# Two decay products ahead of the previous pair's output in a state-space loop

## The chip, the cores and the metric

The kernel runs on one core of one Trainium2 chip. The metric is the device time of one execution in microseconds (us). The engines are TensorE (PE in the rows; PEld is its weight load), VectorE (DVE), ScalarE (ACT), GpSimd (POOL) and SyncE (SP), which issues the weight transfers. Each runs its own instructions in order, and they meet through semaphores.

## The reference, cut to what matters

Two different transformer blocks are computed one after the other, each two layers deep, on 512 positions of width 1024, in float32. Block 1 mixes sliding-window attention, forgetting attention and a state-space part, and then attends to a memory. The change is in the state-space part, in the piece that the reference writes so:

```python
diff = acs[:, :, :, None] - acs[:, :, None, :]
decay = jnp.exp(jnp.where(causal[:, :, None, None], diff, NEG_INF))
cb = jnp.einsum('bclgn,bcsgn->bclsg', cm, bm)
y_diag = jnp.einsum('bclsg,bclsgh,bcsghp->bclghp', cb, decay, xs)
...
y_off = jnp.einsum('bclgn,bcghpn,bclgh->bclghp', cm, prev, jnp.exp(acs))
return (y_diag + y_off).reshape(b, s, h, p)
```

`acs` is a running sum over each chunk of 128 positions, there are 4 chunks and 16 heads of width 64, in two groups of 8. Behind it come the skip term `d_skip * xs` and a gate `silu(z)`.

## The kernel before

The five engines have a program each. In block 1, `first_layer(l)` of each engine runs twice. The state-space loop is `for t in range(HEADS // 2)`: eight turns, one for each pair of heads 2t and 2t+1. It has no scheduler: each engine's order is the order in which its code is written. All sizes are 128 partitions by 512 (4 chunks by 128) for one head, if nothing else is said.

What one turn t does, by engine:

- **TensorE** (from line 2168) waits until the first difference of pair t has been read out of its bank (`spread_read`), then broadcasts the running sums of pair t+1 to all partitions, one head to a bank (`broadcast_sums`, two of them; the banks are 0, 1 and 6 in turn, and the operand has 16 rows), then multiplies four 512 KB units of a weight matrix that has nothing to do with this loop (`mod_unit`, the modulation of block 2, 16 matmul records a unit, 64 in a turn), then waits twice for `operand_ready`, that is for the decay products of both heads, and makes the pair's output (28 matmul records that read `work`, `levels` and `h_sb`) in bank 4 or 5.
- **ScalarE** (lines 2386, 2371 and 2393) takes the exponential of the broadcast sums of both heads into `e_off` (two instructions of 128x384), copies the finished group of modulation rows of turn t-1 out of its bank (line 2371), and then takes the exponential of both heads' differences in place, four instructions of 128x128 for a head, eight in all (line 2393). It begins a head's four when VectorE has made that head's difference.
- **VectorE** makes, for each head of the pair, `c_off` (line 2641: `e_off` times the C matrix, 128x384) and the difference `diff` (line 2643: bank minus the token's own sum, cut at it). Then, if t is not 0, it does `pair_out(t - 1)`, the output of the pair before: line 2625 adds the skip term to bank 4 or 5 and frees the bank, line 2627 multiplies by the gate. Then `decay_keyed` (line 2635) for both heads: the exponential of the difference times `cbm`, into `m_dec`, which TensorE's output matmuls read. The buffers of `e_off` and `diff` are two, one for each head of a pair; those of `c_off` and `m_dec` are four, of which the fourth is in the tile `levels`, so that its rows read `levels<-...`. The eighth pair's output follows behind the loop.

The waits of `decay_keyed` are on `act_output`, which ScalarE raises when a head's four exponentials are done. `pair_out` waits for TensorE's output matmuls of the pair that it treats.

```python
def decay_keyed(hh):
    await_(act_output)
    me.link(V.tensor_tensor(m_dec[hh % 4], diff[:, hh % 2, :], cbm[:, hh // 8, :], ALU.mult), operand_ready)
```

The weights come in one stream of 512 KB units into a ring of eight slots. SyncE issues the load of a slot when TensorE has begun the unit that follows the slot's old one. Behind the loop TensorE goes on with the output projection of block 1, from tiles that are ready since long, and comes to the state-space result only four units later.

Of the kernel before, what the change touches and what calls it, by code (L numbers as in the profile page):

```python
# [51 lines left out]
def build(nc, names, out):  # L52
# [4 lines left out]
    with ctx:  # L57
# [2375 lines left out]
        def _(dve):  # L2433
# [6 lines left out]
            def await_(s):  # L2440
                dve.wait_ge(s, me.nth(s))
# [75 lines left out]
            def first_layer(l):  # L2517
# [105 lines left out]
                def pair_out(t):  # L2623
                    bank_full()
                    me.link(V.scalar_tensor_tensor(out=gtmp, in0=xbc[:, t, :], scalar=par1(l, A_SKIP + t),
                                                   in1=banks[4 + t % 2][:, :], op0=ALU.mult, op1=ALU.add), freed_by_dve)
                    me.link(V.tensor_tensor(y[:, 8 + t, :], y[:, 8 + t, :], gtmp, ALU.mult))
# [5 lines left out]
# [4 lines that stand above are left out]
                for t in range(HEADS // 2):  # L2637
                    for hh in (2 * t, 2 * t + 1):
                        r, g = hh % 2, hh // 8
                        await_(act_output)  # L2640
                        me.link(V.tensor_tensor(c_off[hh % 4][:, P:T], xbc[:, 10 + g, P:T], e_off[:, r, P:T], ALU.mult),
                                wait=False)
                        me.link(V.tensor_tensor(chunked(diff[:, r, :]), chunked(banks[SUM_BANKS[hh % 3]][:, :]), acs_tok(hh),  # L2643
                                                ALU.min), spread_read, wait=False)
                    if t:
                        pair_out(t - 1)
                    for hh in (2 * t, 2 * t + 1):
                        decay_keyed(hh)
                def input_sums(v, sums, last=True):

                    t1, t2, t3, t4 = sums
                    low, high = v[:, 0:4, :], v[:, 4:8, :]
                    me.link(V.tensor_tensor(t1, low[:, :, SECOND], low[:, :, FIRST], ALU.subtract))
                    me.link(V.tensor_tensor(t2, high[:, :, SECOND], t1, ALU.subtract))
                    me.link(V.tensor_tensor(t3, high[:, :, SECOND], low[:, :, SECOND], ALU.subtract), wait=False)
                    me.link(V.tensor_tensor(t4, high[:, :, FIRST], t2, ALU.subtract), operand_ready if last else None)
# [74 lines left out]
            for l in range(DEPTH):  # L2731
                first_layer(l)
# [221 lines left out]
```

How the kernel before makes its waits and increments, by code:

```python
            def link(self, ins, s=None, wait=True):  # L232
                s = s or self.step
                self.done[s.name] = self.done.get(s.name, 0) + 1
                ins.then_inc(s, 1)
                if wait:
                    self.eng.wait_ge(s, self.done[s.name])
# [124 lines left out]
        @block.sync  # L363
# [4 lines left out]
            sp.dma_start(x[:, 0:2, 0:T], x_pairs(names["xT"], 0)).then_inc(x_in[0], 16)
            sp.dma_start(const[:, 0:C_LEVEL], names["consts"][:, 0:C_LEVEL]).then_inc(first_consts_in, 16)
            for n in range(1, 4):
                sp.dma_start(x[:, 2 * n:2 * n + 2, 0:T], x_pairs(names["xT"], n)).then_inc(x_in[n], 16)
            sp.dma_start(par[:, :], names["params"]).then_inc(params_in, 16)
            unit = 0
            for blk, l, phase in ORDER:
                if blk == 2 and l == 0 and phase == "na":
                    sp.wait_ge(memory_read, DEPTH)
                    sp.dma_start(x[:, :, T:ALL], names["ctxT"].rearrange("(k p) t -> p k t", p=P)).then_inc(ctx_in, 16)
                    sp.dma_start(cst(C_TAB, 2 * ALL), names["tables2"]).then_inc(ctx_in, 16)
                for n in range(UNITS[phase]):
                    if phase == "na" and n == 6:
                        sp.wait_ge(table_room, l + 1)
                        if l:
                            sp.dma_start(cst(C_TAB, 2 * ALL), names["tables2"]).then_inc(rope_in, 16)
                        sp.dma_start(work[:, RPB_AT:RPB_AT + RPB_WIDTH], names["bias"][l]).then_inc(table_in, 16)
```

## Time and profile before

| what | value |
|---|---|
| three runs | 3464.1, 3467.82 and 3470.92 us, median 3467.82 us |
| the profiled execution | 3461.59 us, of which the span of its instructions is 3459.8 us |
| TensorE busy | 3284.1 us (95%) |
| VectorE busy | 1147.1 us (33%) |
| ScalarE busy | 973.8 us (28%) |
| GpSimd busy | 330.9 us (10%) |
| bytes moved | 437.69 MB, mean 127 GB/s |
| the state-space loop of layer 0 | from 447.18 us (first `c_off`) to 491.83 us (the last pair's output matmuls are over) |
| that of layer 1 | from 1236.38 us to 1281.51 us |

Times inside the trace are microseconds from the start of the span. The sum below is made against the profiled execution, 3461.59 us.

### The profile page before, as it was taken

The page shows a single profiled execution, that of the slowest core. Times are in us where ns is not written, and L with a number is a line of the kernel's source. Part 1 is how long each engine was busy: PE and PEld are TensorE (multiplying, and loading weights), DVE is VectorE, ACT ScalarE, POOL GpSimd, SP SyncE. Part 2 cuts the span into 40 slices and gives each one's busy share as a digit, 9 for nine tenths or more (in the row PEclk, how much of TensorE's full clock was granted, in tenths as well). Part 3 has the DMA queues.
Part 4 walks back from the last instruction along what each step waited for, and adds up shares of the span by engine and source line. Part 5 has one row for each costly group of instructions (what it writes and reads, how often), then busy time and mean ns, then how long its engine had stood idle before and what let it go on. Part 6 is the DMA issues. An engine that isn't in the chain of part 4 may idle for free.

```text
span 3459.8 us, 46188 instructions
## 1 busy us (share of the span) xinstructions
PE 3284.1 (95%) x19102; PEld 1942.4 (56%) x19102; DVE 1147.1 (33%) x2497; ACT 973.8 (28%) x2072; POOL 330.9 (10%) x336
## 2 busy tenths in 40 slices
PE   8999999999999999999999999979989999997999
PEld 4464457875464456876755777533325756663333
DVE  2224454142224464133352456130002344453011
ACT  1345140111335141114232354121113234442110
POOL 0000002110000002110000064011000000430000
PEclk9999999999999999999999999989999999997999
DMA  4221372312221272422101000169993111014997
GB/s 155 98 74 55 104 264 83 123 44 73 67 80 49 75 297 67 134 68 83 43 25 43 13 2 32 61 233 367 360 335 114 43 32 42 1 62 146 396 409 306
DMA packets 120270, 437.69 MB, mean 127 GB/s; under 512 B 13168, under 2 KB 15344, under 8 KB 119424
## 3 DMA queue, kind: packets, MB, share of 16 engines
q1 hardware_dynamic: 113040, 407.45, 32.3%
q0 software_dynamic: 7024, 27.30, 2.4%
q8 instruction: 153, 2.51, 0.3%
q14 instruction: 53, 0.43, 0.0%
HBM read 422.08 MB, written 12.62 MB: 126 GB/s over the span
## 4 chain that ended last, share of the span: by engine, by line
PE 87%; DVE 5%; DMA 3%; ACT 3%; issue 1%; SPq 0%; POOL 0%; DVEq 0%; ACTq 0%; POOLq 0%
PE bank L1880 85%; DMA ring<-in_stream 2%; PE bank L2025 1%; ACT work L2288 1%; DMA h_sb<-in_stream 1%; PE bank L914 0%; DVE work L2469 0%; DVE work L2471 0%; ACT h_sb L2393 0%; DVE work L1631 0%; DMA work<-in_stream 0%; PE bank L2128 0%; DMA work<-tokens,slot_tok 0%; DVE small L1630 0%; DVE work L2498 0%
## 5 line engine op out<-in xcount | busy, mean ns | idle before, releaser
L1880 PE MATMUL bank<-h_sb,ring 128*128 128x512 f32 (+2 forms) x3104 | 1183.7, 536 | 22.5 <-ACT h_sb L1139 10.8
L1880 PEld LDWEIGHTS bank<-h_sb,ring 128*128 128x128 f32 (+1 forms) x3104 | 570.1, 189 | 533.1 <-issue 487.6
L1880 PE MATMUL bank<-y_sb,ring 128*128 128x512 f32 (+1 forms) x928 | 329.4, 512 | 3.3 <-DVEq L230 3.3
L2248 ACT ACTIVATE work<-bank 128x512 f32<-128x512 f32 (+1 forms) x250 | 124.8, 509 | 709.0 <-PE bank L1880 616.3
L1880 PE MATMUL bank<-work 128*64 128x128 f32 (+6 forms) x1936 | 282.0, 347 | 17.0 <-ACT work L2288 4.7
L1880 PE MATMUL bank<-ring,h_sb 128*128 128x128 f32 (+2 forms) x2144 | 284.8, 311 | 1.4 <-ACT work L1302 0.7
L1880 PEld LDWEIGHTS bank<-y_sb,ring 128*128 128x128 f32 x928 | 175.3, 190 | 151.0 <-issue 138.5
L1880 PEld LDWEIGHTS bank<-ring,h_sb 128*128 128x128 f32 (+2 forms) x2144 | 232.2, 185 | 42.3 <-issue 39.2
L1880 PEld LDWEIGHTS bank<-work 128*64 128x64 f32 (+2 forms) x1936 | 181.7, 163 | 93.7 <-issue 57.4
L1880 PE MATMUL bank<-ring,work 128*64 128x512 f32 (+2 forms) x920 | 223.9, 559 | 4.1 <-DMA ring<-in_stream 4.0
L1880 PE MATMUL bank<-y_sb,work 128*64 128x128 f32 (+3 forms) x984 | 185.3, 435 | 1.0 <-DMA work<-in_stream 0.8
L2288 ACT ACTIVATE work<-work,small 128x256 f32<-128x256 f32 (+4 forms) x188 | 109.0, 580 | 194.2 <-DVEq L230 194.0
L2248 ACT ACTIVATE y_sb<-bank 128x512 f32<-128x512 f32 (+1 forms) x163 | 87.0, 557 | 197.5 <-PE bank L1880 173.9
L1880 PEld LDWEIGHTS bank<-ring,work 128*64 128x64 f32 (+1 forms) x920 | 63.7, 130 | 106.0 <-issue 105.3
L1880 PEld LDWEIGHTS bank<-y_sb,work 128*64 128x64 f32 (+2 forms) x984 | 73.8, 137 | 72.2 <-issue 65.7
L1880 PE MATMUL bank<-work,const 64*128 64x128 f32 (+4 forms) x440 | 101.4, 419 | 6.8 <-DVE h_sb L2643 3.7
L2259 ACT ACTIVATE h_sb<-x_sb 128x1024 f32<-128x1024 f32 (+1 forms) x56 | 47.4, 895 | 206.6 <-DVEq L230 200.6
L2025 PEld LDWEIGHTS bank<-const,work 128*128 128x128 f32 x576 | 68.9, 141 | 58.7 <-issue 39.6
L1880 PE MATMUL bank<-work,y_sb 128*64 128x64 f32 (+1 forms) x400 | 96.1, 391 | 4.4 <-issue 2.9
L1770 POOL TENSOR_TENSOR work<-ring 128x512 f32<-128x512 f32 x14 | 18.5, 1324 | 825.3 <-DMA ring<-in_stream 777.0
L2025 PE MATMUL bank<-const,work 128*128 128x128 f32 x576 | 84.6, 275 | 12.2 <-ACT y_sb L2248 11.4
L1880 PE MATMUL bank<-h_sb,work 128*64 128x128 f32 (+3 forms) x544 | 90.1, 372 | 5.0 <-issue 3.7
(322 smaller groups left out, 3674.7 us busy)
## 6 DMA issues: line engine op xcount, KB each, us to landing
ring<-in_stream SPq DMA_DIRECT2D x578, 512.0 KB, 5.1
y_sb<-in_stream SPq DMA_DIRECT2D x110, 512.0 KB, 7.1
h_sb<-in_stream SPq DMA_DIRECT2D x40, 512.0 KB, 14.9
work<-in_stream SPq DMA_DIRECT2D x20, 512.0 KB, 15.3
work<-in_bias SPq DMA_DIRECT2D x2, 2688.0 KB, 9.8
tokens<-work POOLq DMA_DIRECT2D x10, 512.0 KB, 4.1
work<-forget POOLq DMA_DIRECT2D x2, 1536.0 KB, 7.1
x_sb<-in_xT SPq DMA_DIRECT2D x4, 512.0 KB, 5.9
```

Of the source, the lines that this page charges most:

```text
L1770: me.link(V.tensor_tensor(s3, a11, a21, ALU.subtract), weight_sums)
L1880: return nc.tensor.matmul(o, a, b, start=first, stop=last, skip_group_check=True)
L2025: ins = nc.tensor.transpose(banks[b][:, j * P:(j + 1) * P], scores_in(i - 1, s)[:, kb * P:(kb + 1) * P], ident)
L2248: me.link(A(o, i, func, **kw), freed_by_act, wait=False)
L2259: me.link(A(dst[:, k:k + 2, :], src[:, k:k + 2, :], ACT.Square), squares_ready, wait=False)
L2288: me.link(A(at, banks[s][:, 0:u["nk"]] if raw else at, ACT.Exp, bias=nmax[:, j:j + 1], scale=1.0 if raw else -1.0, accum_out=rsum[:, j:j + ...
```

## The change

Inside a turn of the loop, VectorE's two `decay_keyed` are written ahead of `pair_out(t - 1)` instead of behind it. Nothing is added or removed, and no other engine's program changes. The first turn, which has no `pair_out`, and the part behind the loop stay as they are.

```diff
@@ -2642,10 +2642,10 @@
                         me.link(V.tensor_tensor(chunked(diff[:, r, :]), chunked(banks[SUM_BANKS[hh % 3]][:, :]), acs_tok(hh),
                                                 ALU.min), spread_read, wait=False)
+                    for hh in (2 * t, 2 * t + 1):
+                        decay_keyed(hh)
                     if t:
                         pair_out(t - 1)
-                    for hh in (2 * t, 2 * t + 1):
-                        decay_keyed(hh)
```

VectorE's queue in the second turn (pair 1) of layer 0 and the beginning of the third, before. The bank at the end of an input tells the rows of line 2625 apart (bank 4 is pair 0's output, bank 5 is pair 1's):

```order
L2641 TENSOR_TENSOR levels<-work,h_sb 128x384
L2643 TENSOR_TENSOR h_sb<-bank0,small 128x512
L2625 SCALAR_TENSOR_TENSOR work<-work,par,bank4 128x512
L2627 TENSOR_TENSOR y_sb<-y_sb,work 128x512
L2635 TENSOR_TENSOR work<-h_sb,cpad 128x512
L2635 TENSOR_TENSOR levels<-h_sb,cpad 128x512
L2641 TENSOR_TENSOR work<-work,h_sb 128x384
L2643 TENSOR_TENSOR h_sb<-bank1,small 128x512
```

The same place with the change:

```order
L2641 TENSOR_TENSOR levels<-work,h_sb 128x384
L2643 TENSOR_TENSOR h_sb<-bank0,small 128x512
L2635 TENSOR_TENSOR work<-h_sb,cpad 128x512
L2635 TENSOR_TENSOR levels<-h_sb,cpad 128x512
L2625 SCALAR_TENSOR_TENSOR work<-work,par,bank4 128x512
L2627 TENSOR_TENSOR y_sb<-y_sb,work 128x512
L2641 TENSOR_TENSOR work<-work,h_sb 128x384
L2643 TENSOR_TENSOR h_sb<-bank1,small 128x512
```

The two rows of line 2635 have moved ahead of the two of pair 0's output, and these now stand directly ahead of the next pair's `c_off` and difference.

The end of the loop in layer 0, from the last pair's second difference on, before:

```order
L2643 TENSOR_TENSOR h_sb<-bank0,small 128x512
L2625 SCALAR_TENSOR_TENSOR work<-work,par,bank4 128x512
L2627 TENSOR_TENSOR y_sb<-y_sb,work 128x512
L2635 TENSOR_TENSOR work<-h_sb,cpad 128x512
L2635 TENSOR_TENSOR levels<-h_sb,cpad 128x512
L2625 SCALAR_TENSOR_TENSOR work<-work,par,bank5 128x512
L2627 TENSOR_TENSOR y_sb<-y_sb,work 128x512
```

The same place with the change:

```order
L2643 TENSOR_TENSOR h_sb<-bank0,small 128x512
L2635 TENSOR_TENSOR work<-h_sb,cpad 128x512
L2635 TENSOR_TENSOR levels<-h_sb,cpad 128x512
L2625 SCALAR_TENSOR_TENSOR work<-work,par,bank4 128x512
L2627 TENSOR_TENSOR y_sb<-y_sb,work 128x512
L2625 SCALAR_TENSOR_TENSOR work<-work,par,bank5 128x512
L2627 TENSOR_TENSOR y_sb<-y_sb,work 128x512
```

Here too the last two decay products come first, and the outputs of pairs 6 and 7 (banks 4 and 5) follow each other.

## Rows read from the trace of the kernel before

**Rows 1.** Busy time of the engines, and shares of the chain that ended last
```profile
PE 3284.1 (95%) x19102; PEld 1942.4 (56%) x19102; DVE 1147.1 (33%) x2497; ACT 973.8 (28%) x2072; POOL 330.9 (10%) x336
...
PE 87%; DVE 5%; DMA 3%; ACT 3%; issue 1%; SPq 0%; POOL 0%; DVEq 0%; ACTq 0%; POOLq 0%
```
**Rows 2.** The chain through the loop of layer 0: start us, us, what
```profile
460.14 2.46 ACT h_sb L2393 x8
462.60 0.70 DVE work L2635
...
463.31 0.70 DVE work L2635
...
464.04 0.56 DVE work L2641
464.60 0.61 DVE h_sb L2643
...
465.23 2.46 ACT h_sb L2393 x8
...
472.37 6.84 DMA ring<-in_stream
```
**Rows 3.** VectorE in order of time, pair 2 of layer 0: start us, us, what
```profile
461.09 0.74 DVE L2625 SCALAR_TENSOR_TENSOR work<-work,par,bank 128x512 f32<-128x512 f32 x1
461.86 0.69 DVE L2627 TENSOR_TENSOR y_sb<-y_sb,work 128x512 f32<-128x512 f32 x1
462.59 1.42 DVE L2635 TENSOR_TENSOR work<-h_sb,cpad 128x512 f32<-128x512 f32 x2
```
**Rows 4.** TensorE in order of time, pair 2 and the next broadcasts
```profile
461.75 1.95 PE L1880 MATMUL bank<-ring,cond 128*32 128x128 f32 x64
464.11 0.66 PE L1880 MATMUL bank<-work 128*64 128x128 f32 x8 [0.41 <-DVE work L2635]
...
465.79 1.13 PE L1880 MATMUL bank<-work,const 16*128 16x512 f32 x4
```
**Rows 5.** Stretches, layer 0: us, PE, PEld, DVE, ACT, POOL busy, granted clock, DMA
```profile
444.40:448.40 4.00, 2.12 (x12) 0.49 (x13) 1.22 (x3) 0.89 (x3) 0.00 (x0) 0.90 0.76 270
448.40:453.40 5.00, 5.00 (x61) 3.27 (x65) 4.14 (x8) 3.17 (x10) 0.00 (x0) 0.50 0.28 87
...
458.90:464.00 5.10, 4.69 (x96) 3.52 (x96) 4.96 (x9) 4.03 (x12) 0.00 (x0) 1.00 0.99 373
...
484.60:489.70 5.10, 3.98 (x96) 3.07 (x97) 4.97 (x8) 3.04 (x9) 0.00 (x0) 1.00 1.03 408
```
**Rows 6.** ScalarE and then VectorE in order of time, pair 1 of layer 0
```profile
454.83 2.45 ACT L2393 ACTIVATE h_sb<-h_sb,small 128x128 f32<-128x128 f32 x8
...
457.49 0.69 DVE L2635 TENSOR_TENSOR work<-h_sb,cpad 128x512 f32<-128x512 f32 x1
```
**Rows 7.** ScalarE in order of time, pairs 1 and 2 of layer 1
```profile
1243.94 2.44 ACT L2393 ACTIVATE h_sb<-h_sb,small 128x128 f32<-128x128 f32 x8
...
1249.03 2.45 ACT L2393 ACTIVATE h_sb<-h_sb,small 128x128 f32<-128x128 f32 x8 [0.60 <-DVE h_sb L2643]
```
**Rows 8.** TensorE in order of time, the last pair of layer 0, then of layer 1
```profile
489.58 0.64 PE L1880 MATMUL bank<-ring,cond 128*32 128x128 f32 x16 [0.62 <-DMA ring<-in_stream]
490.15 0.32 PE L1880 MATMUL bank<-work 128*64 128x128 f32 x1
...
492.83 3.70 PE L1880 MATMUL bank<-y_sb,ring 128*128 128x512 f32 x8
...
1279.83 0.32 PE L1880 MATMUL bank<-work 128*64 128x128 f32 x1
```
**Rows 9.** TensorE in order of time, pair 0 of layer 0
```profile
448.40 2.08 PE L1880 MATMUL bank<-work,const 16*128 16x512 f32 x4 [1.84 <-DVE h_sb L2643]
450.41 3.64 PE L1880 MATMUL bank<-ring,cond 128*32 128x128 f32 x64
```
**Rows 10.** A stretch ahead of the loop of layer 1, columns as in rows 5
```profile
1219.00:1226.00 7.00, 5.17 (x61) 2.63 (x59) 5.25 (x9) 0.74 (x2) 0.00 (x0) 1.00 0.56 200
```

## The prediction

> **What bounds the kernel now.** I first read the engines' busy time and the chain that ended last. TensorE is busy for 95% of the span and stands for 87% of the chain; VectorE is 5% of the chain [rows 1]. So nearly everywhere VectorE's order is worth nothing, and the question is whether the loop of the change is one of the exceptions. The chain of waits through that loop says that it is. From 460.14 us it leaves TensorE altogether and goes in a circle: eight exponentials on ScalarE (2.46), two decay products of line 2635 on VectorE, then line 2641 and line 2643 of the next pair's first head, and at 465.23 the next eight exponentials [rows 2]. One circle, 465.23 - 460.14 = 5.09 us, is one pair of heads.
>
> Then VectorE's own timeline, to see whether the circle is tight because of a dependency or because VectorE has no time left. It is both. `pair_out` runs from 461.09 to 462.59, where the first decay product starts [rows 3], and ScalarE ends its eighth exponential at 460.14 + 2.46 = 462.60 [rows 2]. So `pair_out` (1.50 us) lies exactly beside the exponentials, and costs the circle nothing. VectorE's busy time in such a pair is 4.96 of 5.10 us [rows 5]; its work of one pair fills the period.
>
> Who else could set the pace? TensorE is busy 4.69 of 5.10 us [rows 5] and waits 0.41 us for the decay products before the pair's output [rows 4]. The DMA engines are busy at a share of 0.99 in pair 2 and 1.03 in the last pairs [rows 5], the chain goes over to the weight stream at 472.37 [rows 2], and the last modulation unit of the loop waits 0.62 us for it [rows 8]. So three things run within some 0.1 us of each other: VectorE with ScalarE, and, toward the end, the weight stream.
>
> **The change part by part.** No instruction is added or removed, TensorE's, ScalarE's and SyncE's queues are the same, and VectorE's semaphores are awaited in the same order. What moves is 1.50 us of `pair_out`, from ahead of the two decay products to behind them, in seven turns of each of two layers.
>
> *The decay products.* Counted from the start of the exponentials, the first head's are done after half of 2.46, that is 1.23, and its product could start there; the second head's after 2.46. VectorE's second difference ends 461.09 - 460.14 = 0.95 after that start [rows 2, 3]. It then idles 0.28 us, makes the first product (0.70), idles until 2.46, and makes the second (0.72 with the gap behind it, from two neighbouring starts, 463.31 and 464.04). TensorE has both at 3.16 after the start of the exponentials, where before it had them at 464.01 - 460.14 = 3.87 [rows 2, 3]. That is earlier by 0.7 within the turn, and it takes the 0.41 wait away from TensorE.
>
> *pair_out.* It now starts at 3.18 and takes its 1.50 us [rows 3], and only then does the next pair's first head start: from line 2641 to the exponentials 465.23 - 464.04 = 1.19 [rows 2]. The new circle is 2.46 + 0.72 + 1.50 + 1.19 = 5.87 us, against 5.09: longer by 0.78, which is the `pair_out` that has come into it (1.50) less the first product that has gone out of it (0.72). The same from the other side: VectorE has work for the old 5.09 and now idles 0.78 in each turn, because the 1.50 us that bridged its wait for the exponentials have gone elsewhere.
>
> *How many turns count, layer 0.* Pair 0 is unchanged. In pair 1 the exponentials start at 454.83 and take 2.45 [rows 6]; they are held by TensorE's modulation group there, not by VectorE, so this start stays. The second product can start at 457.28, against a first one at 457.49 before [rows 6]. Then 457.28 + 0.72 + 1.50 + 1.19 = 460.69 for pair 2's exponentials, against 460.14 [rows 2]. Five more circles, for pairs 3 to 7, give 460.69 + 5 x 5.87 = 490.04, the second product of pair 7 is ready at 490.04 + 2.46 + 0.70 = 493.20, and TensorE starts behind it by the 0.10 that lies between 464.01 and 464.11 [rows 3, 4]: 493.30. Before, it started at 490.15 [rows 8]. That is **+3.15 us**.
>
> *Layer 1.* Exponentials of pair 1 at 1243.94, of pair 2 at 1249.03 [rows 7]. New: 1243.94 + 2.44 + 0.72 + 1.50 + 1.19 = 1249.79 for pair 2, then 5 x 5.87 = 29.35, then 3.16 and 0.10: 1282.40, against 1279.83 [rows 8]. That is **+2.57 us**.
>
> *What takes no part.* The last `pair_out` of the loop (pair 6) ends about 1.5 us behind the last product, and pair 7's output matmuls take some 1.7 us (490.15 to 491.83, the end in the table of times), so pair 7's output is hardly held. Behind the loop TensorE goes on at once with the projection, eight matmuls of 3.70 us for a unit [rows 8], far slower than the stream brings units, so no DMA wait takes the delay back, and it stays in the end time in full. The stream itself needs 5.10 to 5.2 us for four units in the loop; at 5.87 a pair it is no longer waited for. Its part in the old end is small: VectorE's fifth circle would have given TensorE its operands at about 460.14 + 5 x 5.09 + 3.87 + 0.10 = 489.56 instead of 490.15 [rows 2, 3, 8], so 0.6 us of the loss is hidden already, and this is in the sums above.
>
> Sum: 3.15 + 2.57 = **+5.7 us**. On the profiled execution, 3461.59, this gives 3467.3. That execution lies 6.2 us below the median of the three runs (3467.82), so on the median's footing the forecast is 3467.8 + 5.7 = **3473.5 us**. A change of under 0.2%, 6.9 us, can hardly be told from none in this kernel.
>
> *A rule that points the other way.* The row shows TensorE waiting 0.41 us for line 2635 in a pair [rows 4]. The Trainium skill, Perfetto Trace Analysis, section Identifying Performance Opportunities (Optimization Strategy), says to find the gaps of the engine that limits, look who releases them, and make that dependency start sooner; this change does just that. By that rule the gap goes and the sum is a gain, where the circle of rows 2 makes it a loss.
>
> **The rivals.**
>
> *A. The products reach TensorE sooner and the loop gets shorter.* For it: such a wait stands in two pairs of each layer before the weight stream takes over, at most 0.41 us [rows 4]. Worked out: 2 x 0.41 x 2 = 1.6 us less, 3466.2. Against: it needs the circle of rows 2 not to lengthen, that is, `pair_out` behind the products hidden by something, and in those rows nothing lies beside lines 2641 and 2643 but VectorE itself.
>
> *B. The weight stream paces the loop in both orders.* For it: DMA shares of 0.99 to 1.03 and TensorE's waits for the ring near the end [rows 5, 8]. Then the end of the loop stays where it is: about 0, 3467.8. Against: 5 x 0.78 = 3.9 us more on VectorE is much more than the 0.6 us by which the stream is late.
>
> *C. TensorE's clock falls inside the loop: slower than can be overlooked.* The granted clock fell from 2.4 to 1.2 GHz (1.00 to 0.50) at the loop's beginning, behind a stretch in which TensorE was busy 2.12 of 4.00 us, the last of it a wait of 1.84 [rows 5, 9]. It stayed at 2.4 GHz while TensorE was busy 4.69 of 5.10 [rows 5], and also at 5.17 of 7.00, 74% [rows 10]. With the change TensorE works 4.69 of 5.87, 80%, and its idle time, 1.2 us, is one piece behind the pair's output. The price: at 1.2 GHz the two broadcasts and the modulation group take 2.08 + 3.64 [rows 9] instead of 1.13 + 1.95 [rows 4]. In a middle pair most of that fits into the 1.2 us of slack, over two pairs. It decides when it hits the last pair: TensorE is then 0.5 us late for the output and runs up to 5 us of the projection at half speed, as long as it lasted in rows 5, which costs up to 2.5. With some 2.2 us a layer this gives 5.7 + 4.4 = 10.1, 3477.9. A fall in every pair (2.08 + 3.64 + the output's 1.7 = 7.4 us for a pair) would cost 7 x (7.4 - 5.87) = 10.7 us a layer and end near 3495; the 80% speaks against it.
> The Trainium skill, TensorE: Matmul & The Clock Gate, Part 1, holds that the slow clock is the state at rest and that activity lifts it; that is the mechanism of this rival, and it doesn't say whether 80% in this mix is enough. The rows lean to enough.
>
> **How the numbers follow.** The longer circle with nothing more: chance 0.68, 3473.5, with a range of its own from 3470.5 to 3477 for the drift between executions (the runs spread over 6.8 us). Some of that range lies beyond 6.9 us over the median: of the 0.68 I give 0.48 to no change that can be told and 0.20 to slower. A: 0.07, of which 0.02 would show as faster. B: 0.13, all within 0.2%. C: 0.12, of which 0.11 slower. In all faster 0.02, same 0.67 (0.48 + 0.05 + 0.13 + 0.01), slower 0.31. The range must take in most of C above (3477.9) and B below (3467.8, less a little drift): 3466 to 3480. It leaves out the heavy form of C.
>
> **What would show it.** In the changed trace: VectorE's line 2635 in two separate rows with an idle time of about 0.5 us before the second, put down to ScalarE's line 2393; `pair_out` directly behind it; starts of the eight exponentials 5.87 us apart from pair 2 to pair 7 in both layers, about 490.0 and 1279 plus the shift for the last; no wait of TensorE for line 2635 over 0.2 us, but one of about 1 us before the broadcasts, put down to line 2643; its waits for the ring gone from the last pairs; the DMA share in the loop down to about 0.9. I am wrong if the period is still 5.1 (the exponentials or `pair_out` would have been hidden after all), if the last output matmuls start at the old distance from the loop's start (B), if the granted clock shows 0.5 in a stretch of the loop beyond pair 1 (C), or if the loop is longer by 5 to 6 us in all and the whole is not, which would mean that something later takes it back.

## The result, and the profile after

Over 17 runs the changed kernel took 3475.57 us in the median (3468.44 to 3479.72); 17 runs of the kernel before had a median of 3466.3 us (3458.79 to 3474.45). The ratio is 1.0024 with a 95% interval of 1.0017 to 1.0031: slower by 8.3 us, between 5.9 and 10.7 (the medians themselves are 9.3 us apart). The profiled execution has a span of 3470.6 us, against 3459.8.

The page, with busy times, the chain by engine and the chain by line (what answers to [rows 1]):

```profile
PE 3289.4 (95%) x19102; PEld 1944.6 (56%) x19102; DVE 1148.1 (33%) x2497; ACT 972.5 (28%) x2072; POOL 330.6 (10%) x336
...
PE 87%; DVE 5%; ACT 3%; DMA 2%; issue 1%; SPq 0%; DVEq 0%; POOL 0%; ACTq 0%; POOLq 0%
PE bank L1880 84%; PE bank L2025 1%; ACT h_sb L2393 1%; DMA ring<-in_stream 1%; PE bank L914 1%; DMA h_sb<-in_stream 1%; ACT work L2288 0%; DVE work L2469 0%; DVE work L2471 0%; DVE work L1631 0%; DMA work<-in_stream 0%; DVE small L1630 0%; PE bank L2128 0%; DVE work L2498 0%; DMA work<-tokens,slot_tok 0%
```

The busy times agree with those of before to within 0.2%. In the chain, ScalarE's line 2393, the exponentials of the loop, has come up from 0% to 1%, and DMA has gone from 3% to 2%. The chain of waits through the loop of layer 0 (start us, us, what) shows why, beside [rows 2]:

```profile
459.78 2.45 ACT h_sb L2393 x8
462.24 0.03 issue
462.26 0.02 DVEq L2441
462.28 0.04 issue
462.33 0.70 DVE work L2635
...
463.05 0.76 DVE work L2625
...
463.84 0.70 DVE y_sb L2627
...
464.56 0.56 DVE work L2641
465.12 0.61 DVE h_sb L2643
...
465.76 2.45 ACT h_sb L2393 x8
...
493.01 33.32 PE bank L1880 x118
```

The circle holds one decay product instead of two, and both instructions of `pair_out`. One turn is 465.76 - 459.78 = 5.98 us, against 5.09. It goes round like this up to pair 7, without passing over to the weight stream. What the prediction's circle did not have are the first three lines under the exponentials: 0.09 us from ScalarE's end to VectorE's start.

VectorE in order of time in the same pair (start us, us, engine, line, operation; idle before in brackets), against [rows 3]:

```profile
461.09 0.69 DVE L2635 TENSOR_TENSOR work<-h_sb,cpad 128x512 f32<-128x512 f32 x1 [0.28 <-ACT h_sb L2393]
462.33 0.69 DVE L2635 TENSOR_TENSOR work<-h_sb,cpad 128x512 f32<-128x512 f32 x1 [0.55 <-ACT h_sb L2393]
463.05 0.75 DVE L2625 SCALAR_TENSOR_TENSOR work<-work,par,bank 128x512 f32<-128x512 f32 x1
463.84 0.69 DVE L2627 TENSOR_TENSOR y_sb<-y_sb,work 128x512 f32<-128x512 f32 x1
```

The two products are apart, with idle times of 0.28 and 0.55 us, both put down to line 2393. Their sum, 0.83, is the greater part of the 0.89 us by which a turn is longer.

TensorE (as [rows 4] and [rows 8]): the next broadcasts, the output of pair 3, and the output of the last pair:

```profile
465.78 1.13 PE L1880 MATMUL bank<-work,const 16*128 16x512 f32 x4 [0.91 <-DVE h_sb L2643]
...
469.10 0.29 PE L1880 MATMUL bank<-work 128*64 128x128 f32 x1 [0.31 <-DVE levels L2635]
...
493.01 0.29 PE L1880 MATMUL bank<-work 128*64 128x128 f32 x1 [1.36 <-DVE levels L2635]
```

The wait for the products shrinks only from 0.41 to 0.31, and a wait of 0.91 for the next difference has come, which was not there before. Why the first shrinks so little, the broadcasts of pair 2 in the kernel before show:

```profile
460.69 1.13 PE L1880 MATMUL bank<-work,const 16*128 16x512 f32 x4
```

They began 0.55 us after the exponentials (460.14); now they begin 0.02 us after them (465.78 and 465.76). The output matmuls start 3.34 us after the exponentials instead of 3.97, so the products do come 0.63 us sooner within the turn, but TensorE is there sooner too, by 0.53. The last pair's output starts at 493.01, not at 490.15. It waits for line 2635 for 1.36 us, and no longer for the ring.

The stretches of the loop (columns as in [rows 5]):

```profile
448.40:453.40 5.00, 5.00 (x76) 3.41 (x78) 4.14 (x8) 3.46 (x11) 0.00 (x0) 0.66 0.36 110
459.80:465.80 6.00, 4.78 (x98) 3.55 (x98) 5.07 (x9) 3.72 (x12) 0.00 (x0) 1.00 0.98 366
...
483.70:489.70 6.00, 4.77 (x99) 3.54 (x99) 5.07 (x9) 3.72 (x12) 0.00 (x0) 1.00 0.98 378
```

TensorE's work of a turn, 4.8 us, is now spread over 6.0, and the granted clock stays at 1.00 all the same. But in the first stretch it is 0.66 here, where [rows 5] have 0.50. This becomes important below. Layer 1 has the same turns:

```profile
1248.60 2.45 ACT L2393 ACTIVATE h_sb<-h_sb,small 128x128 f32<-128x128 f32 x8
1254.58 2.45 ACT L2393 ACTIVATE h_sb<-h_sb,small 128x128 f32<-128x128 f32 x8 [1.49 <-DVE h_sb L2643]
...
1284.46 2.44 ACT L2393 ACTIVATE h_sb<-h_sb,small 128x128 f32<-128x128 f32 x8 [2.28 <-DVE h_sb L2643]
...
1287.81 0.29 PE L1880 MATMUL bank<-work 128*64 128x128 f32 x1 [1.37 <-DVE levels L2635]
```

From here on "the loop's length" is measured from the start of pair 0's exponentials to the start of pair 7's output matmuls. Before it is 490.15 - 448.38 = 41.77 us in layer 0 and 1279.83 - 1237.58 = 42.25 in layer 1; with the change 493.01 - 448.36 = 44.65 and 1287.81 - 1242.18 = 45.63. By this one pair of profiles the two loops cost 6.3 us.

### The profile page after: what moved, and what is told of

Read it like the earlier page. It is cut to its first block, busy times and chain, and to the rows that moved or that the text cites. A ratio compares the mean times of both kernels' runs of the same rounds, so it can differ in the third digit from the quotient of the medians.

```text
span 3470.6 us, 46188 instructions
## 1 busy us (share of the span) xinstructions
PE 3289.4 (95%) x19102; PEld 1944.6 (56%) x19102; DVE 1148.1 (33%) x2497; ACT 972.5 (28%) x2072; POOL 330.6 (10%) x336
## 4 chain that ended last, share of the span: by engine, by line
PE 87%; DVE 5%; ACT 3%; DMA 2%; issue 1%; SPq 0%; DVEq 0%; POOL 0%; ACTq 0%; POOLq 0%
PE bank L1880 84%; PE bank L2025 1%; ACT h_sb L2393 1%; DMA ring<-in_stream 1%; PE bank L914 1%; DMA h_sb<-in_stream 1%; ACT work L2288 0%; DVE work L2469 0%; DVE work L2471 0%; DVE work L1631 0%; DMA work<-in_stream 0%; DVE small L1630 0%; PE bank L2128 0%; DVE work L2498 0%; DMA work<-tokens,slot_tok 0%
## 5 line engine op out<-in xcount | busy, mean ns | idle before, releaser
L1880 PE MATMUL bank<-h_sb,ring 128*128 128x512 f32 (+2 forms) x3104 | 1185.1, 536 | 22.5 <-ACT h_sb L1139 10.8
L2025 PE MATMUL bank<-const,work 128*128 128x128 f32 x576 | 84.5, 275 | 11.4 <-ACT y_sb L2248 10.7
```

The costliest lines, as they stand in the source:

```text
L1880: return nc.tensor.matmul(o, a, b, start=first, stop=last, skip_group_check=True)
L2025: ins = nc.tensor.transpose(banks[b][:, j * P:(j + 1) * P], scores_in(i - 1, s)[:, kb * P:(kb + 1) * P], ident)
```

## The experiments

Two questions stood open: which part of the new order costs, and why 8.3 us were measured where the loops show 6.3. Lengths and turns of all profiles are in this table, and all differences of code below are shown against the kernel before. A turn is the distance of two pairs' exponentials in pairs 2 to 7 (the median of them); totals are against runs of the kernel before on the same chip, from the ratio and its 95% interval.

| kernel | turn | loop, layer 0 | loop, layer 1 | total against before |
|---|---|---|---|---|
| before, three profiles | 5.1 to 5.2 | 41.77, 42.24, 41.98 | 42.25, 40.72, 42.17 | |
| the change, three profiles | 5.98 | 44.65, 45.66, 45.65 | 45.63, 45.66, 45.67 | +8.3 (5.9 to 10.7) |
| `pair_out` between the products | 5.46 | 42.57 | 43.58 | +5.5 (2.1 to 9.0) |
| `pair_out` in halves | 5.20 to 5.25 | 42.06 | 41.13 | -1.4 (-4.9 to +2.1) |
| change in layer 0 alone | 5.98, 5.09 | 44.64 | 40.05 | +8.3 (4.5 to 11.8) |
| old order, a product twice | 5.82 | 45.04 | 45.96 | +15 (9 to 21) |
| old order, no gate | 5.1 (4.61 at first) | 40.07 | 40.67 | +1.0 (-3.5 to +5.5) |
| changed order, no gate | 5.25 | 40.47 | 41.71 | +1.7 (-2.8 to +5.9) |
| old order, gap filled | 5.1 | 41.96 | 40.43 | -2.4 (-5.5 to +0.3) |
| changed order, gap filled | 5.97 | 43.67 | 43.66 | +6.9 (3.8 to 10.4) |

### pair_out between the two products

```diff
+                    decay_keyed(2 * t)
                     if t:
                         pair_out(t - 1)
-                    for hh in (2 * t, 2 * t + 1):
-                        decay_keyed(hh)
+                    decay_keyed(2 * t + 1)
```

> pair_out stands between the two decay products. Theory 1 (the circle: whatever stands on VectorE behind the second head's exponentials, up to the next pair's first difference, lengthens the pair) expects: first product 1.31 us after the start of the exponentials (as the changed kernel's trace has it), then 0.72, pair_out 1.50, second product at 3.53, and with 0.73 and 1.19 a pair of 5.45 us; the last pair's output starts 1.7 us later than before in layer 0 and 1.1 us in layer 1, +2.9 us in all. Theory 2 (the products moved ahead are not what costs, a later stage takes the loss) expects the loop near +6 as with the whole change, since one product still goes first. Rival (VectorE's work alone sets the pair): 5.1 us a pair, +0.5 at most.

VectorE in order of time in one turn:

```profile
461.92 0.69 DVE L2635 TENSOR_TENSOR work<-h_sb,cpad 128x512 f32<-128x512 f32 x1 [0.28 <-ACT h_sb L2393]
462.64 0.75 DVE L2625 SCALAR_TENSOR_TENSOR work<-work,par,bank 128x512 f32<-128x512 f32 x1
463.43 0.69 DVE L2627 TENSOR_TENSOR y_sb<-y_sb,work 128x512 f32<-128x512 f32 x1
464.15 0.69 DVE L2635 TENSOR_TENSOR work<-h_sb,cpad 128x512 f32<-128x512 f32 x1
...
467.38 0.69 DVE L2635 TENSOR_TENSOR work<-h_sb,cpad 128x512 f32<-128x512 f32 x1 [0.28 <-ACT h_sb L2393]
```

The turn is 467.38 - 461.92 = 5.46, where 5.45 was expected. The idle time of 0.28 before the first product is left, that of 0.55 before the second is gone, and the turn is 0.52 shorter than with the whole change. So each of the two idle times has its place: the first comes from putting a product ahead of `pair_out`, the second from putting both. The rival that only VectorE's work counts (5.1 us a turn) falls.

### pair_out in halves

Its first instruction (line 2625) ahead of the products, the gate behind them. The gate gets a function of its own, `pair_gated`, which is called for the eighth pair behind the loop as well (not shown):

```diff
                     if t:
                         pair_out(t - 1)
                     for hh in (2 * t, 2 * t + 1):
                         decay_keyed(hh)
+                    if t:
+                        pair_gated(t - 1)
```

> pair_out is cut in two: its first instruction (skip term, frees the bank) stands ahead of the products, the second (gate) behind them. Circle theory: the first instruction (0.77) covers VectorE's wait for the first head's exponentials, first product at 1.74, second at 2.48, gate 0.72, then 1.19: 5.11 to 5.18 us a pair, with idle time on VectorE under 0.1. The second product is ready 0.7 us earlier in the turn than before, but the weight stream releases the last pair's modulation group at the old time: the loop ends within 0.5 us of before in both layers, total 0 to +1. If simply having products ahead of any output work costs, +3 or more.

Two lines are added to the file ahead of it, so that line 2635 is now 2637 and the gate 2629:

```profile
463.24 0.74 DVE L2625 SCALAR_TENSOR_TENSOR work<-work,par,bank 128x512 f32<-128x512 f32 x1
464.01 1.52 DVE L2637 TENSOR_TENSOR work<-h_sb,cpad 128x512 f32<-128x512 f32 x2
465.57 0.69 DVE L2629 TENSOR_TENSOR y_sb<-y_sb,work 128x512 f32<-128x512 f32 x1
466.30 0.56 DVE L2643 TENSOR_TENSOR work<-work,h_sb 128x384 f32<-128x384 f32 x1
...
468.44 0.73 DVE L2625 SCALAR_TENSOR_TENSOR work<-work,par,bank 128x512 f32<-128x512 f32 x1
```

One turn is 468.44 - 463.24 = 5.20. Half of `pair_out` is enough to bridge the wait for the first head, and the second product costs only the 0.1 us of a start that waits (the two products take 1.52 together, 1.42 in [rows 3]). Half of the output work behind the products is thus nearly free; what costs is VectorE standing still. Against before nothing can be told (-4.9 to +2.1): this order is no improvement that the runs can show.

### The change in layer 0 alone

```diff
-                    if t:
+                    if t and l:
                         pair_out(t - 1)
                     for hh in (2 * t, 2 * t + 1):
                         decay_keyed(hh)
+                    if t and not l:
+                        pair_out(t - 1)
```

> The change in layer 0 alone. Circle theory: +2.9 us in layer 0's loop (measured 2.88 with the whole change), 0 in layer 1's, total about +3, a third to a half of the whole change's +8.3. If the part of +8.3 that the two loops don't hold (6.3) is made later in the program by the shift, then this kernel too shows more than its loop, +4 or over; if it is drift between executions, +3.

The loop of layer 0 is that of the whole change to 0.01 us (44.64 against 44.65). The surprise is in layer 1, whose loop has the old order and took 40.05 us where the first profile had 42.25. TensorE in order of time at its beginning:

```profile
1244.93 1.21 PE L1880 MATMUL bank<-work,const 16*128 16x512 f32 x4 [1.84 <-DVE h_sb L2643]
1246.07 3.48 PE L1880 MATMUL bank<-ring,cond 128*32 128x128 f32 x64
```

The broadcasts take 1.21 us here, 2.08 in [rows 9]. The idle time of 1.84 is the same, but the granted clock was at 1.2 GHz for a shorter piece of this beginning: over the first 5.0 us of the loop its mean is 0.66, where [rows 5] have 0.50. So the first profile's starts were slow ones, and the old order's length goes with the start by up to 2 us. Some 1.0 us of that is the start of pair 1's exponentials (5.43 us behind pair 0's here, 6.36 and 6.45 in the first profile). The rest goes with TensorE's waits for the weight stream, which are 1.3 us in this loop and 1.8 and 2.4 in those of the first profile. The total, +8.3 (4.5 to 11.8), is more than the +3 that was expected; it is taken up again below.

### A product made twice

The order of before, and ahead of the two products one more that makes the first head's values, overwritten by the same values right behind:

```diff
                     if t:
                         pair_out(t - 1)
+                        await_(act_output)
+                        me.awaited[act_output.name] -= 1
+                        me.link(V.tensor_tensor(m_dec[2 * t % 4], diff[:, 0, :], cbm[:, t // 4, :], ALU.mult))
                     for hh in (2 * t, 2 * t + 1):
                         decay_keyed(hh)
```

> The order of before, and the first head's decay product made twice (0.72 us more VectorE work a turn in seven turns of two layers, the first making is overwritten by the same values). It measures what a us of delay in this circle costs in the end. Circle theory: 5.09 + 0.72 = 5.81 us a pair; pair 7's output starts 4.4 us later in layer 0, 3.7 in layer 1, total +8.1. If the weight stream paced the loop: +0 to +2. If a delayed loop costs more later: over +10.

The turn is 5.82 us, 0.01 off. VectorE has no time left in the old order: an instruction of 0.72 us more makes every turn 0.73 longer. The total is +15 (9 to 21), from six runs that lie between 3473.1 and 3491.91 us.

### The gate left out, in both orders

In both kernels the multiplication of line 2627 is left out for pairs 0 to 6, so their output isn't multiplied by silu(z). The first has the old order, the second the changed one; only the call of `pair_gated` behind the loop is left.

> The order of before, with the gate multiplication (line 2627, 0.69 us) of pairs 0 to 6 left out: their output isn't multiplied by silu(z). VectorE then has 4.3 us of work a pair. If the circle (exponentials, two products, next difference) is what sets the pair, nothing changes: 5.09 us a pair in pairs 2 and 3, with about 0.7 us of VectorE idle before line 2635; total 0. If VectorE's work sets it, 4.4 us a pair in pairs 2 and 3, and then the weight stream at 5.1 to 5.2; total -1 at most.

VectorE in the old order without the gate:

```profile
463.19 0.75 DVE L2625 SCALAR_TENSOR_TENSOR work<-work,par,bank 128x512 f32<-128x512 f32 x1
463.97 1.52 DVE L2637 TENSOR_TENSOR work<-h_sb,cpad 128x512 f32<-128x512 f32 x2
465.52 0.56 DVE L2643 TENSOR_TENSOR work<-work,h_sb 128x384 f32<-128x384 f32 x1
...
467.90 0.75 DVE L2625 SCALAR_TENSOR_TENSOR work<-work,par,bank 128x512 f32<-128x512 f32 x1
```

This turn is 467.90 - 463.19 = 4.71 us; pairs 2 and 3 have 4.61 and 4.71, in layer 1 4.61 and 4.62. Expected by the circle theory were 5.09. That theory, as it was put, is wrong for the old order: the first head's product needs only the first head's exponentials and runs beside the second's. The 5.09 of before was VectorE's own work. The 4.6 us are not the dependency either, but TensorE's work. It goes through these turns without an idle time, and ScalarE waits for TensorE's bank ahead of the exponentials:

```profile
463.07 1.13 PE L1880 MATMUL bank<-work,const 16*128 16x512 f32 x4
464.13 2.04 PE L1880 MATMUL bank<-ring,cond 128*32 128x128 f32 x64
...
467.78 1.13 PE L1880 MATMUL bank<-work,const 16*128 16x512 f32 x4
```

```profile
461.53 0.60 ACT L2371 ACTIVATE h_sb<-bank 128x512 f32<-128x512 f32 x1 [0.70 <-PE bank L1880]
462.25 2.45 ACT L2393 ACTIVATE h_sb<-h_sb,small 128x128 f32<-128x128 f32 x8
```

So this run shows only that the dependency allows 4.61 or less. An estimate from the changed kernel's chain is 4.5 (its turn of 5.98 less the 1.50 of `pair_out`). From pair 4 on the turn is 5.1 to 5.5, and the DMA engines' share in 480 to 490 us is 1.03: there the weight stream sets it. The two loops together are 3.0 us shorter than on the mean of before (41.86 us a loop, worked out below), but the total shows no change that can be told.

> The changed order, with the same gate multiplication of pairs 0 to 6 left out. Circle theory: what is left out stands in the circle here, so the pair falls from 5.98 to 5.25 us, and since 6 x 5.25 nearly keeps up with the stream, the loop ends within 1 us of before: total 0 to +1 against before, about 7 less than the changed kernel. If the loss of the change comes from where TensorE or the stream stand and not from pair_out's length, it stays at +5 to +8.

VectorE in the changed order without the gate:

```profile
462.20 0.69 DVE L2637 TENSOR_TENSOR work<-h_sb,cpad 128x512 f32<-128x512 f32 x1 [0.55 <-ACT h_sb L2393]
462.93 0.75 DVE L2625 SCALAR_TENSOR_TENSOR work<-work,par,bank 128x512 f32<-128x512 f32 x1
...
467.45 0.69 DVE L2637 TENSOR_TENSOR levels<-h_sb,cpad 128x512 f32<-128x512 f32 x1 [0.55 <-ACT h_sb L2393]
```

467.45 - 462.20 = 5.25 us, as expected. Here what is left out comes off the turn in full (5.98 - 0.73), and the idle time of 0.55 stays. So in the changed order `pair_out` stands in the dependency, and its length counts one to one. The loop is back at 40.47 and 41.71, and the total at +1.7 (-2.8 to +5.9).

### Both orders once more, for their starts

The two kernels as they are, two more profiles of each.

> The kernel before once more, for a second profile. The clock theory: the loop's length from pair 0's exponentials to pair 7's output matmuls depends in the old order on how long the granted clock stays at 0.50 at its beginning: 40.0 to 40.3 us where the stretch at 0.50 is 3.4 us (as in layer 1 of the kernel with the change in layer 0 alone, 40.05), 41.8 to 42.3 where it is longer (as in the first profile, 41.77 and 42.25). Rival: the loop's length doesn't depend on it and 40.05 was something else.

> As the run before it: a third profile of the old order, same two values for the loop's length by its clock. From the ends of the loops to the end of the program both should agree with the first profile but for half of the difference in time at clock 0.50.

> The changed kernel once more. The pair is 5.98 us whatever the clock at the beginning, which moves pair 1's start alone: 44.65 us with the short stretch at 0.50, 45.63 with the longer one. So the change costs 4.6 a layer where both start with the short stretch, and 3.4 to 3.9 with the long one, 7 to 9 us in all, not the 6.3 that the first two profiles give.

> As the run before it: a third profile of the new order, 44.65 or 45.63 us a loop by its clock.

The changed order gave 45.65 to 45.67 in all four loops, the value for the long stretch at the low clock. The old order gave 42.24, 41.98 and 42.17, and once, with a short stretch, 40.72 (40.0 to 40.3 had been expected, so a short start is worth 1.3 to 2 us there, not always 2). The means over three profiles are 41.86 for the old loop and 45.49 for the new: 3.63 us a layer, **7.3 us in both**. The first profile of the changed kernel had a short start in layer 0, by chance, and that is why the first pair of profiles showed 6.3. TensorE waits for the weight stream in every old loop (1.7 to 2.5 us in these six), in the changed ones only once in six, for 0.8 us.

Outside the loops the executions differ more than this: the span less both loops is 3375.8, 3384.6 and 3384.3 us for the old kernel and 3380.3, 3387.4 and 3388.5 for the changed one. The third profile's expectation, that the old kernel's executions would nearly agree from the loops' ends on, failed: from pair 7's output matmuls in layer 1 to the end they took 2180.0, 2187.5 and 2188.5 us. On the mean of three the changed kernel's rest is 3.8 us longer. Of this, 3.0 lie ahead of the loop of layer 0, where the two kernels are the same (450.64 against 447.67 us up to pair 0's exponentials), 1.0 between the loops, and nothing behind that of layer 1 (2185.2 against 2185.3). So these profiles show no later cost of the change.

### The gap at the beginning filled

Three of pair 0's four modulation units are written ahead of TensorE's first wait for a difference, in the old order and in the changed one:

```diff
+                for n in range(3):
+                    mod_unit(4 * EARLY_GROUPS + n)
                 for t in range(HEADS // 2):
                     pe.wait_ge(spread_read, HEADS * l + 2 * t + 1)
...
-                    for n in range(4):
+                    for n in range(0 if t else 3, 4):
```

> The order of before, and three of pair 0's four modulation units stand on TensorE ahead of its wait for the first difference, where all traces show it idle for 1.84 us and the granted clock falls. If that gap is what drops the clock and starts the stream late, the clock stays at 1.00 (or drops for less), pair 1's exponentials follow pair 0's by about 4.5 us instead of 5.3 to 6.4, the stream is no longer waited for at the end, and the loop is 6 x 5.09 + 4.0 + 4.5 = 39.0 us long instead of 41.6 on the mean: -2.5 to -3 a layer, -5 to -6 in all. If the clock falls anyway, 0 to -2.

TensorE at the beginning of layer 0's loop, old order, and the stretches there:

```profile
451.80 0.66 PE L1880 MATMUL bank<-work 128*64 128x128 f32 x8 [1.62 <-DVE work L2637]
...
454.49 2.08 PE L1880 MATMUL bank<-work,const 16*128 16x512 f32 x4
```

```profile
448.00:452.00 4.00, 1.99 (x28) 0.90 (x26) 3.14 (x6) 3.54 (x11) 0.00 (x0) 1.00 0.92 281
452.00:456.00 4.00, 4.00 (x32) 2.65 (x28) 3.33 (x6) 2.58 (x9) 0.00 (x0) 0.55 0.65 257
```

The clock now holds through the first gap, but a wait of 1.62 us for pair 0's products has taken its place, and behind it the clock falls (0.55) and the next broadcasts take 2.08. The gap was moved, not filled: loops of 41.96 and 40.43 instead of the 39.0 expected, and -2.4 us (-5.5 to +0.3), which is not clear of nothing. In layer 1 the clock falls at the same place.

> The same three units ahead, in the changed order. Circle theory: the pair stays 5.98 us; the loop is 4.5 + 6 x 5.98 + 3.35 = 43.7 us, 4.7 a layer more than the old order with the same start: about +9 us against the run before it, +4 against before. So with a start that is the same in both, and no stream to wait for, the change costs its full price. If the changed order's loss came from the start or from the stream, the two are alike.

The loops are 43.67 and 43.66, the 43.7 expected, although the clock was low for a while in layer 0 and stayed at 1.00 in layer 1: where VectorE's circle paces from pair 0 on, TensorE has the slack to hide it. Against the old order with the same three units ahead the two loops are 4.9 us longer, and the medians differ by 3474.59 - 3466.30 = 8.3 us.

### What stays open

Every delayed kernel's total lies above the sum of its loops: +8.3 against 7.3 for the change, +5.5 against 2.4 (42.57 and 43.58 less twice 41.86), +8.3 against 1.0 or, with a start of the common kind in layer 1, 2.8; +15 against 7.3; 8.3 against 4.9 for the pair with the gap filled. The intervals of the kernel with one layer changed and of that with the product twice exclude their own sums; that of the change itself does not. It isn't a matter of delay alone: the two kernels without the gate have loops that are 3.0 and 1.5 us shorter than twice 41.86, and totals of +1.0 and +1.7, though with intervals that take in their sums.

A part of the excess may be the clock, in some of these kernels. Among 29 runs of the kernel before in one comparison, time and mean granted clock correlate at -0.90 (in the others at -0.73 to -0.78), and among the 17 of the changed one a fit gives 0.58 us for each us of lost clock (one less the mean clock, times the span). The mean clock was 0.9775 in the runs with one layer changed, with `pair_out` between and with the product twice, and 0.9785 in those of before: 0.001 x 3470 x 0.58 = 2 us, an estimate. For the change itself it explains nothing that shows: its 17 runs have a mean clock of 0.9791, and the runs of before in the four comparisons 0.9785 to 0.9792. Whether a loop that ends later makes the clock fall more often behind it, or whether this is chance, the runs don't tell, and where the excess is made stays open.

## Why the prediction was right or wrong

**What bounds the loop: half right.** The chain does leave TensorE in this loop and go round between ScalarE and VectorE, and the loop's time does reach the end. But "It is both" (dependency and work) was wrong. The old turn of 5.09 us was VectorE's work alone: with 0.72 us more it rose by 0.73, and without the gate it fell to 4.61, where TensorE's work set it. I took ScalarE's end at 462.60 and `pair_out`'s end at 462.59 for a dependency, though the first product waits only for the first head's exponentials, over since about 461.37 (half of 2.46 behind 460.14). So `pair_out` beside the exponentials wasn't free either. This changed no term of the sum, since the new circle was rightly built.

**The products 0.7 us earlier: right, and worth nothing,** as forecast. The wait that was to vanish (0.41) only shrank to 0.31, where at most 0.2 was forecast. The prediction left TensorE where it was in the turn, but counted from the exponentials it now comes to its broadcasts 0.53 us sooner. And the output matmuls start 3.34 us after the exponentials, 0.08 later than the 3.16 + 0.10 forecast, since VectorE has to wait for ScalarE.

**The new circle, 5.87 us: 5.98 measured.** This is the term that was mis-sized. Its parts were right (2.45 + 0.72 + 1.50 + 1.19), but the hand-over from ScalarE to an idle VectorE was missing, 0.03 + 0.02 + 0.04 = 0.09 in the chain. At this place the rows of before couldn't show it, because VectorE came to the second product from work of its own. But the chain of before has it ahead of the loop, where VectorE does wait for ScalarE:

```profile
447.09 0.03 issue
447.12 0.02 DVEq L2441
447.14 0.04 issue
```

In six circles of two layers the 0.11 that was missing makes 1.3 us.

**How many circles, and from where: right in number.** Layer 0 was forecast to end at 493.30 and ended at 493.01, only because its start fell on the short stretch of low clock; with the common start it is one us later (45.65 against the forecast 493.30 - 448.38 = 44.92). Forecast +3.15 and +2.57, on the mean +3.63 each: 5.7 against 7.3 in the loops and 8.3 (5.9 to 10.7) in the whole.

**What takes no part: right.** `pair_out` of pair 6 ended at 494.41, and pair 7's began at 494.86. The stream was no longer waited for, and nothing behind the loop gave time back.

**The rule on gaps.** The Trainium skill's advice in Perfetto Trace Analysis, to make the dependency of the limiting engine's gap start sooner, was followed by the change, and did make it start sooner; the gap turned up 2 us further on at the next wait (0.91 us for line 2643). The engine to read was VectorE.

**The rivals.** A (a gain) fell: no profile of the changed kernel has a turn under 5.97 in pairs 2 to 7. B (the stream paces both) fell for the changed order, but the stream does set the old order's last pairs, as the kernels without the gate show. C (the clock falls inside the loop) didn't come: 1.00 in all later stretches at 80% busy. The clock mattered where I had not priced it, in the first pair, and it works against the old order: a low start goes with up to 2 us there, waits for the stream included, and with only 1.0 in the changed one.

**The numbers.** 3473.5 was forecast, 3475.57 measured, inside 3466 to 3480. Of the classes, 0.67 went to a change that can't be told and 0.31 to a slower one; measured was +0.24% (0.17 to 0.31), most likely in the second, though the interval takes in the line between them. The time fits better than the change does: 3467.8, the median of three runs that the forecast started from, lay 1.5 us above the 3466.3 of all 17. By chance that made up for a part of the 5.7 us forecast against 8.3, and 5.7 lies just below the interval. With the 0.09 us for each wake in the circle the sum would have stood at 7, on the border, and the chances at about even.

## What to carry to other kernels

When an engine alternates between waiting for a partner and work that can go anywhere, keep the free work where the wait is. It costs nothing there up to the length of the wait (0.83 us here, so that by the estimate of 4.5 above some 0.9 of the 1.50 of `pair_out` was free); behind the last thing that the partner needs it stands in the dependency and counts in full. The consumer's short wait (0.41 us here) is no reason to move a product ahead if the engine that makes it then stands still for longer (0.83). Before calling a turn bound by a dependency, write down for each instruction which single producer it needs: an engine with hardly any idle time may be bound by its work, even if a partner happens to end at the same moment.

## What the runs showed of the hardware

- A VectorE instruction that is waiting for ScalarE starts 0.09 us after ScalarE's end (0.03 + 0.02 + 0.04 in the chain). One that VectorE reaches after its own work, with the semaphore already raised, starts 0.02 to 0.03 after the one before it.
- Ahead of the loop's second pair of broadcasts TensorE is idle for 1.84 us in every profile of a kernel without the filled gap, in both layers, and each time the granted clock falls to 1.2 GHz. It falls during the idle time (0.50 in the last us of it in a profile of the old order) or only in the broadcasts behind it (0.95 in their first us and 0.50 in the next, in layer 1 of the kernel with one layer changed). The old order's loops took 40.05 to 42.25 us, the shorter ones with the shorter stretch of low clock. Three units of work put into that gap kept the clock up there. At the next gap, of 1.62 us, it fell in three of four loops and stayed at 1.00 in the fourth. The Trainium skill (TensorE: Matmul & The Clock Gate, Part 1) has the slow clock as the state at rest, and calls the point at which it lifts variable from run to run. The falls beside idle time fit the first; the traces add that the fall varies too.
- Two executions of one kernel differed by more outside the loops (3375.8 and 3384.6 us) than the change was worth. A single pair of profiles (+10.8 us in the span) would have been a poor measure of it.
